# The later modulation products of a diffusion backbone, row sums on VectorE and one matmul per unit on TensorE

## The chip, the core and the metric

The kernel runs on one core of one Trainium2 chip. The metric is the device time of one execution in microseconds (us). Before the change the median of 3 runs is 3228.99 us (3227.17 to 3229.79). Everything is float32. The engines are TensorE (PE), VectorE (DVE), ScalarE (ACT), GpSimd (POOL) and SyncE (SP); POOL and SP here mostly issue DMAs.

## The reference, cut to what matters

Two layers, each a mixer and a mixture of single-neuron experts ("PEER") over 512 latent tokens of width 1024; layer 0's mixer also reads 256 context tokens. Every sub-layer is modulated by a shift, a scale and a gate that come from the conditioning vector:

```python
silu_c = jax.nn.silu(c)                       # c: (1, 1024)
for l in range(DEPTH):                        # DEPTH = 2
    sh1, sc1, g1, sh2, sc2, g2 = jnp.split((silu_c @ ada_w[l] + ada_b[l])[:, None, :], 6, axis=-1)
    h = modulate(x, sh1, sc1)                 # rms_norm(x) * (1 + sc1) + sh1
    ...                                       # even: attention and spatial gating; odd: convolution
    x = x + g1 * y
    x = x + g2 * peer_ffn(modulate(x, sh2, sc2), peer_wq[l], peer_keys[l], peer_down[l], peer_up[l])
```

`ada_w[l]` is 1024 by 6144. So the modulation is a product of one row of 1024 numbers with 2 times 25 MB of weights (`c_ctx` needs a part of layer 0's as well). `peer_ffn` picks 128 experts for each token and gathers their down and up rows (1024 numbers each); that is most of the kernel's DMA.

## The kernel before, in words

**Stages.** The plan (`make_plan`, L520) writes one order of stage phases; each engine walks it and takes from it its own part (`run_phases`, L757). Ahead of the first expert gather stands the front, some 270 us: norms and projections of all tokens, layer 0's mixer for block 0 (128 tokens), the choice of its experts, and the whole modulation. Then come 8 stretches of 128 gathers (4 blocks, 2 layers), with the other blocks' mixers and choices spread between them (`beside`, L422). The order in the front is the text `FRONT` (L512): a word is a stage's letter and a phase. `k`, `q` and `v` are projections, `g` the gating, `a` the attention (23 phases of `ATTEND`, L458), `p` the output projection and the update of x, `n` the norm for the experts, `s` the choice of experts, `u` and `w` modulation products and `t` and `y` their transposition. Inside the front all engines have the same order.

**Modulation.** The weights come in halves: 512 columns of 512 of the 1024 rows, 1 MB, in SBUF as 128 partitions of 4 rows by 512 columns. Two halves are a unit (`unit`, L182), which is 512 outputs of one section; a section has 1024 outputs, so 2 units. There are three groups of units (`side`, L195): 4 units for the first norms, 6 (`u`), and the last 14 units, 28 halves, `w0` to `w27` in `FRONT`. GpSimd issues the halves' DMAs in order (L823), five to eight ahead: the DMA for a half waits on the count `side_used`, which says how many products have been read out of the buffers. For a half TensorE runs 4 matmuls (L1595), one for each of the 4 rows, into the 4 groups of 32 output partitions, with `cond_slide` as the stationary operand: 32 columns of zeros with the conditioning numbers in two of them, moved so that unit m adds to row 2m of each group. After the last half ScalarE copies the 128 by 512 sums to SBUF (`turned`, L889), TensorE sums the four groups and transposes in one (4 matmuls with `chosen`, L1607) and VectorE adds the biases (L1215).

**What is around it.** `attend` on VectorE takes row maxima of the scores (`peaks`, L1312) and mixes the two softmaxes (`combine`, L1319); ScalarE waits for the first with its exponentials and TensorE for the second with a transposition. `gating` on VectorE: `bn_stats` (L1287), the normalisation (L1292 to L1296) and the product (L1303). `project` on VectorE: two passes of 1024 columns (L1354, L1356) that update x; ScalarE then squares and sums x, VectorE takes the reciprocal (L1228), scales x (L1229), TensorE transposes, VectorE and ScalarE modulate one half each (L1236, L958). After that TensorE starts the choice's projections (L1578), and the first gathers follow.

Of the kernel before, what the change touches and what calls it, by code (L numbers as in the profile page):

```python
# [18 lines left out]
ALU = mybir.AluOpType  # L19
# [3 lines left out]
P = 128  # L23
# [90 lines left out]
class Plan:  # L114
# [80 lines left out]
    def side(self, sections):  # L195

        units = [self.unit(layer, sec, j, 2 * n + j) for n, (layer, sec) in enumerate(sections) for j in range(2)]
        sums = Stage("side", parts=units, cost=(1,) * (2 * len(units)))
        turned = Stage("turned", parts=sections, cost=(1, 1))
        sums.group = turned.group = self.groups  # L200
# [315 lines left out]
p3 p4 p5 n0 w24 w25 n1 w26 w27 n2 y0 n3 s0 y1 s1 s2 s3 s4 s5 s6 s7  # L516
# [3 lines left out]
def make_plan():  # L520
# [46 lines left out]
    rest, rest_turned = p.side([(1, SH1), (1, SC1), (1, G1), (1, SH2), (1, SC2), (1, G2), (0, G2)])  # L567
# [24 lines left out]
def trunk_kernel(nc, A, out):  # L592
    plan = make_plan()
    with ExitStack() as ctx:
# [58 lines left out]
        diag = sb("diag", [P, RING, HALF])  # L653
        psum = ctx.enter_context(nc.psum_tensor("psum", [P, 4, 2 * COLS], F32))
# [69 lines left out]
        side_used, side_line = sem("side_used"), sem("side_line")  # L724
        side_out, side_done = sem("side_out"), sem("side_done")
# [133 lines left out]
        def _(act):  # L859
# [277 lines left out]
        def _(dve):  # L1137
# [26 lines left out]
            dve.memset(cond_slide, 0.0).then_inc(consts, 1)  # L1164
            dve.wait_ge(first_params, 48)
# [25 lines left out]
            def lam(s):  # L1191
# [9 lines left out]
                                              op0=ALU.add, op1=ALU.subtract))  # L1201
                yield
# [318 lines left out]
            run_phases({"turned": turned, "front_norms": front_norms, "lam": lam, "norm": norm, "heads": heads, "gating": gating, "attend": attend, "project": project,  # L1521
# [4 lines left out]
        def _(pe):  # L1526
# [54 lines left out]
            def side(s):  # L1581
# [4 lines left out]
                elif s.group == 2:  # L1586

                    pe.wait_ge(side_line, 1)
# [9 lines left out]

            def turned(s):
# [268 lines left out]
```

## Time and profile before

| | us |
|---|---|
| median of 3 runs | 3228.99 (3227.17 to 3229.79) |
| span of the profiled execution (first to last instruction) | 3226.1 |
| its own run time | not listed apart from the three runs |
| TensorE busy | 2352.4 (73%) |
| VectorE busy | 2215.5 (69%) |
| ScalarE busy | 1284.6 (40%) |
| GpSimd busy | 1194.8 (37%) |
| DMA, 1286.05 MB | mean 399 GB/s |

The span runs from the first to the last instruction; the median of the runs stands 2.9 us above it. Busy shares are averages over unlike stages: the front is short, 8% of the span, and has other limits than the gathers. The chain that ended last is 33% DMA, 31% TensorE, 20% VectorE and 8% ScalarE.

### The profile page before, as it was taken

How to read it: one execution, taken by the hardware profiler on the slowest of the kernel's cores; microseconds unless marked ns; L12 is line 12 of the kernel's file. 1: busy time of each engine (PE TensorE's matmuls, PEld its weight loads, DVE VectorE, ACT ScalarE, POOL GpSimd, SP SyncE). 2: the span in 40 equal slices, each digit the busy share in tenths (PEclk: the TensorE clock that was granted, in tenths of full speed). 3: DMA queues.
4: the chain of work that ended last, by engine and by line, in shares of the span. 5: the costliest groups of instructions: out<-in, count | busy, mean ns of one | idle time of the engine just before them, and what ended most of it. 6: DMA issues, size and time to landing. Idle time of an engine off the chain costs nothing.

```text
span 3226.1 us, 38561 instructions
## 1 busy us (share of the span) xinstructions
PE 2352.4 (73%) x13032; PEld 919.0 (28%) x13032; DVE 2215.5 (69%) x5652; ACT 1284.6 (40%) x3707; POOL 1194.8 (37%) x1076
## 2 busy tenths in 40 slices
PE   6997778576775878876685796956686667867776
PEld 2335225122341235431151251511143112511110
DVE  2325875866568655869849968599948996795444
ACT  3223463345434553533434534333343433443333
POOL 1102343433334342335433434335433453344332
PEclk9998789688887888887797796967688667966666
DMA  8778999999999999999999999999999999999998
GB/s 333 260 300 344 415 375 423 410 398 406 410 422 414 418 401 421 391 422 410 419 404 416 401 418 420 392 404 397 421 399 421 405 421 391 421 399 422 421 421 357
DMA packets 169766, 1286.05 MB, mean 399 GB/s; under 512 B 19552, under 2 KB 20448, under 8 KB 23392
## 3 DMA queue, kind: packets, MB, share of 16 engines
q0 software_dynamic: 154368, 1124.14, 85.4%
q1 hardware_dynamic: 15200, 159.45, 11.9%
q8 instruction: 102, 1.67, 0.2%
q14 instruction: 96, 0.79, 0.1%
HBM read 1281.42 MB, written 2.10 MB: 398 GB/s over the span
## 4 chain that ended last, share of the span: by engine, by line
DMA 33%; PE 31%; DVE 20%; ACT 8%; issue 7%; POOL 1%; DVEq 0%; SPq 0%; ACTq 0%; POOLq 0%
DMA ring<-in_experts,expert 32%; PE psum L1798 11%; DVE ring L1500 8%; PE psum L1564 7%; PE psum L1578 4%; PE psum L1744 4%; DVE arena L1391 2%; PE psum L1536 1%; PE psum L1595 1%; ACT shares_of L1128 1%; ACT diag L1129 1%; DVE arena L1419 1%; PE psum L1550 1%; ACT acts L1127 1%; ACT L1127 1%
## 5 line engine op out<-in xcount | busy, mean ns | idle before, releaser
L1798 PE MATMUL psum<-ring,diag 64*64 64x512 f32 x8192 | 1430.3, 805 | 746.7 <-ACT diag L1129 739.8
L852 POOL DMA_INDIRECT ring<-in_experts,expert x1024 | 1169.0, 1142 | 1807.0 <-PE psum L1798 1666.0
L1500 DVE CUSTOM_DVE_ANT_0 ring<-ring,h 128x1024 f32<-128x1024 f32 x1024 | 1230.9, 1223 | 530.3 <-DMA ring<-in_experts,expert 499.9
L1127 ACT ACTIVATE acts<-dots 128x1 f32<-128x1 f32 x1024 | 206.7, 202 | 1475.0 <-DVE dots L1500 1431.4
L1798 PEld LDWEIGHTS psum<-ring,diag 64*64 64x64 f32 x8192 | 286.4, 162 | 1719.5 <-ACT diag L1129 1519.6
L1129 ACT ACTIVATE diag<-ident_half,shares_of 128x64 f32<-128x64 f32 x1024 | 356.4, 348 | 33.3
L1128 ACT ACTIVATE shares_of<-acts,gate 128x1 f32<-128x1 f32 x1024 | 302.0, 295 | 33.3
L1391 DVE SCALAR_TENSOR_TENSOR arena<-kept,taps,arena 128x128 f32<-128x128 f32 x960 | 262.6, 345 | 0.1
L1578 PEld LDWEIGHTS psum<-arena,weights 128*128 128x128 f32 x2048 | 234.2, 192 | 48.9 <-issue 47.0
L1578 PE MATMUL psum<-arena,weights 128*128 128x128 f32 x2048 | 245.7, 278 | 0.1
L878 ACT ACTIVATE arena<-psum 128x512 f32<-128x512 f32 (+1 forms) x105 | 65.5, 624 | 206.0 <-PE psum L1578 119.6
L1564 PE MATMUL psum<-weights,arena 128*128 128x512 f32 x272 | 135.5, 644 | 4.7 <-ACTq L962 4.7
L1744 PE MATMUL psum<-arena,weights 128*128 128x256 f32 x512 | 119.1, 386 | 0.4 <-ACTq L962 0.4
L1564 PE MATMUL psum<-weights,ring 128*128 128x512 f32 x240 | 112.2, 612 | 3.7 <-ACTq L917 3.7
L1536 PE MATMUL psum<-ident,arena 128*128 128x128 f32 x464 | 81.2, 328 | 35.4 <-DVEq L1396 8.1
L1744 PEld LDWEIGHTS psum<-arena,weights 128*128 128x128 f32 x512 | 94.6, 190 | 38.6 <-issue 24.4
L1127 ACT ACT_TABLE_LOAD x78 | 100.1, 1283 | 6.0 <-ACT arena L1034 2.0
L833 POOL DMA_DIRECT2D ring<-in_chunks x46 | 24.5, 535 | 198.4 <-PE psum L1595 167.8
L1536 PEld LDWEIGHTS psum<-ident,arena 128*128 128x128 f32 x464 | 64.0, 168 | 101.5 <-issue 50.1
L1316 DVE TENSOR_REDUCE peak<-psum 128x1 f32<-128x768 f32 x32 | 30.5, 952 | 80.6 <-PE psum L1691 80.4
L1500 DVE DVE_READ_ACCUMULATOR2_ANT dots<- 128x1 f32 x1024 | 84.1, 82 | 0.0
L1564 PEld LDWEIGHTS psum<-weights,arena 128*128 128x128 f32 x272 | 53.3, 207 | 86.4 <-issue 80.0
(166 smaller groups left out, 1519.3 us busy)
## 6 DMA issues: line engine op xcount, KB each, us to landing
weights<-in_chunks SPq DMA_DIRECT2D x70, 2048.0 KB
ring<-in_chunks POOLq DMA_DIRECT2D x46, 1024.0 KB, 7.2
ring<-in_experts,expert POOLq DMA_INDIRECT x1024
arena<-in_chunks SPq DMA_DIRECT2D x10, 512.0 KB
x<-in_x SPq DMA_DIRECT2D x1, 2048.0 KB, 19.8
kept<-in_chunks POOLq DMA_DIRECT2D x2, 1024.0 KB, 19.9
out_x<-x SPq DMA_DIRECT2D x4, 512.0 KB
ring<-in_ctx SPq DMA_DIRECT2D x1, 1024.0 KB, 9.6
```

What stands on the lines that cost most here:

```text
L852: pool.indirect_dma_start(out=ring[:, k, :], out_offset=None, in_=table, in_offset=bass.IndirectOffsetOnAxis(ap=expert[:, s.b % 2, n:n + 1 ...
L878: step(act.activation(dst, src, ACT.Copy))
L1127: step(act.activation(acts[:, k:k + 1], dots[:, k:k + 1], ACT.Gelu))
L1128: step(act.activation(shares_of[:, k:k + 1], acts[:, k:k + 1], ACT.Copy, scale=gate[:, s.b % 2, n:n + 1]))
L1129: act.activation(diag[:, k, :], ident_half[:], ACT.Copy, scale=shares_of[:, k:k + 1]).then_inc(diag_ready, 1)
L1391: dve.scalar_tensor_tensor(out=acc[:, k, :], in0=z_t[:, k, w + s.b * P:w + (s.b + 1) * P], scalar=taps[:, k, w:w + 1], in1=acc[:, k, :], o ...
L1500: dve.tensor_tensor_reduce(out=ring[:, k, 0:D], in0=ring[:, k, 0:D], in1=h2[:, s.b % 2, :], scale=1.0, scalar=0.0, op0=ALU.mult, op1=ALU.a ...
L1536: ins = pe.transpose(psum[:, t.bank, k * P:(k + 1) * P], src[:, k * P:(k + 1) * P], ident[:])
L1564: ins = pe.matmul(dst, left[:, k, :], buffers[c.buf][:, k, :], start=k == 0 and begin, stop=k == KD - 1, skip_group_check=not begin)
L1578: ins = pe.matmul(dst, buffers[c.buf][:, k, g * P:(g + 1) * P], right[:, k, :], start=k == 0, stop=k == KD - 1)
L1744: ins = pe.matmul(psum[:, t.bank, 2 * g * P:2 * (g + 1) * P], buffers[c.buf][:, k, g * P:(g + 1) * P], h_pair[:, k, :], start=k == 0, stop ...
L1798: pe.matmul(ffn_out[rows_out, r * COLS:(r + 1) * COLS], diag[rows_in, k, :], ring[rows_in, k, D + n * COLS:D + (n + 1) * COLS], start=Fals ...
```

## The change

The last group's 28 halves are no longer multiplied on TensorE. VectorE keeps one 128 by 512 tile per unit: it multiplies the first row of the first half with the conditioning number of each partition (one `tensor_scalar`) and adds the other seven rows, each times its number (seven `scalar_tensor_tensor`). Each of these waits for the one before it through `side_used`, which GpSimd waits on too. There are two such tiles, a new one and the tile `diag`, which is not in use before the gathers. When a unit is whole, TensorE adds up the partitions with one matmul of 32 output rows (`one_slide`: zeros with a column of ones) into the bank. The stage has 30 phases in place of 28: TensorE's matmul for unit m stands in phase 2m + 3, VectorE's work for the unit's halves in phases 2m and 2m + 1. At the end ScalarE copies 32 rows in place of 128 and TensorE transposes with 32 rows of the identity. The first two groups stay as they are.

```diff
-    def side(self, sections):
+    def side(self, sections, added=False):
+        before = len(self.units)
         units = [self.unit(layer, sec, j, 2 * n + j) for n, (layer, sec) in enumerate(sections) for j in range(2)]
-        sums = Stage("side", parts=units, cost=(1,) * (2 * len(units)))
+        sums = Stage("added" if added else "side", parts=units, cost=(1,) * (2 * len(units) + (2 if added else 0)))
...
-p3 p4 p5 n0 w24 w25 n1 w26 w27 n2 y0 n3 s0 y1 s1 s2 s3 s4 s5 s6 s7
+p3 p4 p5 n0 w24 w25 n1 w26 w27 n2 w28 w29 y0 n3 s0 y1 s1 s2 s3 s4 s5 s6 s7
...
-    rest, rest_turned = p.side([(1, SH1), (1, SC1), (1, G1), (1, SH2), (1, SC2), (1, G2), (0, G2)])
+    rest, rest_turned = p.side([(1, SH1), (1, SC1), (1, G1), (1, SH2), (1, SC2), (1, G2), (0, G2)], added=True)
...
+        one_slide = sb("one_slide", [P, 62])
+        added_to = [sb("added_to", [P, COLS])[:], diag[:].rearrange("p s n -> p (s n)")]
...
             def turned(s):
-                act.wait_ge(side_used, s.used)
                 if s.group == 2:
                     act.wait_ge(side_out, 1)
-                act.activation(lines[s.group], side_bank[s.group], ACT.Copy).then_inc(side_line, 1)
+                    act.wait_ge(side_summed, s.added)
+                    act.activation(lines[s.group][0:32, :], side_bank[s.group][0:32, :], ACT.Copy).then_inc(side_line, 1)
+                else:
+                    act.wait_ge(side_used, s.used)
+                    act.activation(lines[s.group], side_bank[s.group], ACT.Copy).then_inc(side_line, 1)
...
+            def added(s):
+                dve.wait_ge(cond_act, 1)
+                used = s.before
+                for u in s.parts:
+                    dst = added_to[u.m % 2]
+                    if u.m > 1:
+                        dve.wait_ge(side_summed, u.m - 1)
+                    for h, (buf, there, _) in enumerate(u.halves):
+                        dve.wait_ge(side_landed[buf], there)
+                        for k in range(KD // 2):
+                            dve.wait_ge(side_used, used)
+                            share = cond_slide[:, 4 * h + k, 30:31]
+                            if h + k == 0:
+                                ins = dve.tensor_scalar(dst, side_bufs[buf][:, k, :], share, None, ALU.mult)
+                            else:
+                                ins = dve.scalar_tensor_tensor(out=dst, in0=side_bufs[buf][:, k, :], scalar=share, in1=dst,
+                                                               op0=ALU.mult, op1=ALU.add)
+                            ins.then_inc(side_used, 1)
+                            used += 1
+                        if h:
+                            dve.wait_ge(side_used, used)
+                            dve.sem_inc(side_added, 1)
+                        yield
+                yield
+                yield
...
+            def added(s):
+                yield
+                yield
+                yield
+                pe.wait_ge(side_line, 1)
+                pe.wait_ge(one_ready, 2)
+                for u in s.parts:
+                    at = 30 - 2 * u.m
+                    pe.wait_ge(side_added, u.m + 1)
+                    pe.matmul(side_bank[s.group][0:32, :], one_slide[:, at:at + 32], added_to[u.m % 2], start=u.m == 0,
+                              stop=True, skip_group_check=True).then_inc(side_summed, 1)
+                    yield
+                    yield
...
+                rows, turn_by = (32, ident[0:32, 0:32]) if s.added else (P, chosen[:])
                 for g in range(4):
-                    ins = pe.matmul(dst[:, 32 * g:32 * (g + 1)], lines[s.group][:, g * P:(g + 1) * P], chosen[:], start=True, stop=True)
+                    ins = pe.matmul(dst[:, 32 * g:32 * (g + 1)], lines[s.group][0:rows, g * P:(g + 1) * P], turn_by, start=True, stop=True)
```

How this moves the instructions is seen at three places. In the rows `waits` names the counts that an instruction waits for; the new kernel's lines on VectorE stand 40 further down than the old ones (L1316 is L1356 there), and its `added` is L1231 and L1233.

First, VectorE around the last pair of score maxima of the front's attention. Before, from the gating's statistics to the gating's product:

```order
L1287 BN_STATS stats<-psum 128x6 [waits psum_full1]
L1288 BN_AGGR meanvar<-stats 128x2 [waits dve_step]
L1292 RECIPROCAL rstd_v<-std_v 128x1 [waits std_ready]
L1293 TENSOR_SCALAR g2_row<-psum,meanvar,rstd_v 128x512 [waits dve_step]
L1295 TENSOR_TENSOR g2_row<-g2_row,vn_gain 128x512 [waits dve_step]
L1296 TENSOR_TENSOR g2_row<-g2_row,vn_gain 128x512 [waits dve_step]
L1316 TENSOR_REDUCE peak<-psum 128x1 [waits psum_full0]
```

Now the same stretch from the end of the gating's normalisation, up to the gating's product:

```order
L1336 TENSOR_TENSOR g2_row<-g2_row,vn_gain 128x512 [waits dve_step]
L1233 SCALAR_TENSOR_TENSOR diag<-ring,arena,diag 128x512 [waits side_used,side_landed0]
L1233 SCALAR_TENSOR_TENSOR diag<-ring,arena,diag 128x512 [waits side_used] x3
L1356 TENSOR_REDUCE peak<-psum 128x1 [waits side_used,psum_full0]
L1357 TENSOR_SCALAR neg_peak<-peak 128x1 [waits dve_step]
L1356 TENSOR_REDUCE peak<-psum 128x1 [waits psum_full1]
L1357 TENSOR_SCALAR neg_peak<-peak 128x1 [waits dve_step]
L1231 TENSOR_SCALAR added_to<-ring,arena 128x512 [waits side_used,side_landed1,side_summed]
L1233 SCALAR_TENSOR_TENSOR added_to<-ring,arena,added_to 128x512 [waits side_used] x3
L1362 RECIPROCAL inv_sum<-expsum 128x2 [waits exp_ready]
```

Four operations (half `w19`) now stand ahead of the maxima, and four (`w20`) between the maxima and the mix.

Second, VectorE from the update of x to the modulation of the experts' input. Before:

```order
L1356 TENSOR_TENSOR x<-x,arena 128x1024 [waits dve_step]
L1228 RECIPROCAL rstd<-std 128x1 [waits std_ready]
L1229 TENSOR_SCALAR arena<-x,rstd 128x1024 [waits dve_step]
L1236 TENSOR_SCALAR arena<-psum,mod 128x128 [waits mod_ready,psum_full2]
L1236 TENSOR_SCALAR arena<-psum,mod 128x128 x3
```

Now:

```order
L1396 TENSOR_TENSOR x<-x,arena 128x1024 [waits dve_step]
L1231 TENSOR_SCALAR added_to<-ring,arena 128x512 [waits side_used,side_landed0,side_summed]
L1233 SCALAR_TENSOR_TENSOR added_to<-ring,arena,added_to 128x512 [waits side_used] x3
L1233 SCALAR_TENSOR_TENSOR added_to<-ring,arena,added_to 128x512 [waits side_used,side_landed1]
L1233 SCALAR_TENSOR_TENSOR added_to<-ring,arena,added_to 128x512 [waits side_used] x3
L1268 RECIPROCAL rstd<-std 128x1 [waits side_used,std_ready]
L1269 TENSOR_SCALAR arena<-x,rstd 128x1024 [waits dve_step]
L1231 TENSOR_SCALAR diag<-ring,arena 128x512 [waits side_used,side_landed2,side_summed]
L1233 SCALAR_TENSOR_TENSOR diag<-ring,arena,diag 128x512 [waits side_used] x3
L1233 SCALAR_TENSOR_TENSOR diag<-ring,arena,diag 128x512 [waits side_used,side_landed3]
L1233 SCALAR_TENSOR_TENSOR diag<-ring,arena,diag 128x512 [waits side_used] x3
L1276 TENSOR_SCALAR arena<-psum,mod 128x128 [waits side_used,mod_ready,psum_full2]
```

Eight operations (`w24`, `w25`) now stand between the update of x and the reciprocal, and eight (`w26`, `w27`) between the scaled x and its modulation.

Third, TensorE around the scores of head 2 (L1691 before, L1744 now). Before:

```order
L1595 MATMUL psum<-ring,arena 32x512 [waits side_landed8]
L1595 MATMUL psum<-ring,arena 32x512 x3
L1691 MATMUL psum<-kept,arena 128x512 [waits psum_free0]
L1691 MATMUL psum<-kept,arena 128x256
L1691 MATMUL psum<-kept,arena 128x512 [waits psum_free1]
L1691 MATMUL psum<-kept,arena 128x256
L1595 MATMUL psum<-ring,arena 32x512 [waits side_landed0]
L1595 MATMUL psum<-ring,arena 32x512 x3
L1707 MATMUL psum<-kept,arena 128x128 [waits psum_free2,probst_ready,v_ready]
```

Now:

```order
L1646 MATMUL psum<-diag,one_slide 32x512 [waits side_added]
L1744 MATMUL psum<-kept,arena 128x512 [waits psum_free0]
L1744 MATMUL psum<-kept,arena 128x256
L1744 MATMUL psum<-kept,arena 128x512 [waits psum_free1]
L1744 MATMUL psum<-kept,arena 128x256
L1760 MATMUL psum<-kept,arena 128x128 [waits psum_free2,probst_ready,v_ready]
```

Four matmuls for every half became one for every second half, and it waits for VectorE (`side_added`) where the four waited for a DMA (`side_landed`).

## Rows read from the trace of the kernel before

**Rows 1.** Busy time in four stretches: length, engines, granted TensorE clock, DMA share, GB/s.
```profile
117.00:184.50 67.50, 65.92 (x272) 25.86 (x270) 11.71 (x25) 13.77 (x23) 7.42 (x14) 1.00 0.71 253
184.50:238.00 53.50, 50.67 (x240) 23.32 (x242) 14.29 (x29) 14.11 (x23) 4.77 (x9) 1.00 0.80 322
238.00:290.00 52.00, 37.75 (x300) 30.98 (x300) 18.19 (x62) 12.03 (x23) 9.35 (x9) 0.90 0.74 294
290.00:3226.00 2936.00, 2111.34 (x11888) 803.28 (x11880) 2135.22 (x5453) 1211.72 (x3571) 1159.65 (x1015) 0.78 0.99 409
```

**Rows 2.** Chain of waits, front: start us, us, what.
```profile
117.41 1.85 PE psum L1595 x16
...
178.44 3.63 PE psum L1564 x8
...
222.49 1.00 PE psum L1595 x8
...
228.45 1.00 PE psum L1595 x8
```

**Rows 3.** VectorE's groups by shape, first 290 us: busy us, mean ns of one.
```profile
L1270 DVE TENSOR_TENSOR arena<-arena,rope_cos 128x512 f32<-128x512 f32 x5 | 3.5, 691 | 0.2
L1174 DVE TENSOR_SCALAR arena<-x,rstd 128x1024 f32<-128x1024 f32 x4 | 2.7, 748 | 0.0
...
L1198 DVE TENSOR_SCALAR subln<-subln 128x128 f32<-128x128 f32 x1 | 0.2, 217 | 0.0
```

**Rows 4.** The page's costliest groups, the convolution's taps.
```profile
L1391 DVE SCALAR_TENSOR_TENSOR arena<-kept,taps,arena 128x128 f32<-128x128 f32 x960 | 262.6, 345 | 0.1
```

**Rows 5.** VectorE in order of time: start us, us, what, idle before.
```profile
197.00 0.70 DVE L1287 BATCH_NORM_STATS2 stats<-psum 128x6 f32<-128x512 f32 x1 [7.31 <-PE psum L1564]
...
198.28 0.16 DVE L1292 RECIPROCAL rstd_v<-std_v 128x1 f32<-128x1 f32 x1 [0.36 <-ACT std_v L1016]
198.47 0.81 DVE L1293 TENSOR_SCALAR g_row<-psum,meanvar,rstd_v 128x512 f32<-128x512 f32 x1
199.43 0.69 DVE L1295 TENSOR_TENSOR g_row<-g_row,vn_gain 128x512 f32<-128x512 f32 x1
...
208.73 0.96 DVE L1316 TENSOR_REDUCE peak<-psum 128x1 f32<-128x768 f32 x1 [7.88 <-PE psum L1691]
...
213.92 0.17 DVE L1322 RECIPROCAL inv_sum<-expsum 128x2 f32<-128x2 f32 x1 [2.99 <-ACTq L1038]
...
214.37 1.02 DVE L1325 SCALAR_TENSOR_TENSOR arena<-arena,inv_sum 128x768 f32<-128x768 f32 x1
215.31 1.12 DVE L1303 SCALAR_TENSOR_TENSOR arena<-psum,sgu_bias,g_row 128x128 f32<-128x128 f32 x4
225.57 0.69 DVE L1336 TENSOR_TENSOR arena<-arena 128x512 f32<-128x512 f32 x1 [9.14 <-ACTq L1053]
...
227.35 0.18 DVE L1341 RECIPROCAL rstd<-std 128x4 f32<-128x4 f32 x1 [0.37 <-ACT std L1056]
...
239.38 1.23 DVE L1356 TENSOR_TENSOR x<-x,arena 128x1024 f32<-128x1024 f32 x1
242.15 0.16 DVE L1228 RECIPROCAL rstd<-std 128x1 f32<-128x1 f32 x1 [1.54 <-ACT std L949]
...
244.29 1.37 DVE L1236 TENSOR_SCALAR arena<-psum,mod 128x128 f32<-128x128 f32 x4 [1.19 <-PE psum L1536]
```

**Rows 6.** TensorE in order of time, the same columns.
```profile
217.27 1.25 PE L1536 MATMUL psum<-ident,arena 128*128 128x128 f32 x10
...
229.38 0.66 PE L1536 MATMUL psum<-ident,arena 128*128 128x128 f32 x4
...
245.99 1.09 PE L1536 MATMUL psum<-ident,arena 128*128 128x128 f32 x8 [1.74 <-ACTq L962]
```

**Rows 7.** GpSimd's DMAs of the halves, line 833.
```profile
DMA to landing us min/median/max: 5.1/7.8/23.7
```

**Rows 8.** GpSimd's first gather, in order of time, the same columns.
```profile
270.06 0.99 POOL L852 DMA_INDIRECT ring<-in_experts,expert  x1 [45.65 <-issue]
```

More of the change, by code:

```diff
@@ L193, in unit @@
         return u
-    def side(self, sections):
+    def side(self, sections, added=False):
+        before = len(self.units)
         units = [self.unit(layer, sec, j, 2 * n + j) for n, (layer, sec) in enumerate(sections) for j in range(2)]
-        sums = Stage("side", parts=units, cost=(1,) * (2 * len(units)))
+        sums = Stage("added" if added else "side", parts=units, cost=(1,) * (2 * len(units) + (2 if added else 0)))
         turned = Stage("turned", parts=sections, cost=(1, 1))
+        sums.before, turned.added = 8 * before, len(units) if added else 0
         sums.group = turned.group = self.groups
@@ L724, in trunk_kernel @@
         side_used, side_line = sem("side_used"), sem("side_line")
+        one_ready = sem("one_ready")
+        side_added, side_summed = sem("side_added"), sem("side_summed")
         side_out, side_done = sem("side_out"), sem("side_done")
@@ L1164, in _ @@
             dve.memset(cond_slide, 0.0).then_inc(consts, 1)
+            dve.memset(one_slide[:], 0.0).then_inc(one_ready, 1)
+            dve.wait_ge(one_ready, 1)
+            dve.memset(one_slide[:, 30:31], 1.0).then_inc(one_ready, 1)
             dve.wait_ge(first_params, 48)
@@ L1519, in finish @@
                 yield
-            run_phases({"turned": turned, "front_norms": front_norms, "lam": lam, "norm": norm, "heads": heads, "gating": gating, "attend": attend, "project": project,
+            run_phases({"added": added, "turned": turned, "front_norms": front_norms, "lam": lam, "norm": norm, "heads": heads, "gating": gating, "attend": attend, "project": project,
                         "conv_in": conv_in, "conv": conv, "select": select, "gather": gather, "finish": finish}, "others")
@@ L1585, in side @@
                     pe.wait_ge(side_done, 1)
-                elif s.group == 2:
-                    pe.wait_ge(side_line, 1)
                 bank = side_bank[s.group]
@@ L1805, in _ @@
             pe.wait_ge(consts, 4)
-            run_phases({"side": side, "turned": turned, "front_norms": front_norms, "norm": norm, "heads": heads, "values": values, "gate_row": gate_row, "gating": gating, "attend": attend,
+            run_phases({"side": side, "added": added, "turned": turned, "front_norms": front_norms, "norm": norm, "heads": heads, "values": values, "gate_row": gate_row, "gating": gating, "attend": attend,
                         "project": project, "conv_in": conv_in, "conv": conv, "select": select, "gather": gather}, "pe")
```

## The prediction

> **What bounds the kernel now.** I read the busy time by stretch first [rows 1]. From 290 us to the end the DMA share is 0.99: the gathers set the pace there, and the change doesn't touch them. So it can only move the time at which they start. In the front the DMA share is 0.71 to 0.80, while TensorE is busy for 65.92 of 67.50 us and 50.67 of 53.50: it bounds the front to about 205 us. VectorE is busy for 11.71 and 14.29 us in the same two stretches. TensorE's granted clock is 1.00 in both, its upper level, so there is no clock to win back. Then I read the chain of waits [rows 2]: between 117 and 230 us the products of the halves stand on it, w0 and w1 as one piece of 1.85 us, 18 pieces of 1.00 (w2 to w19), and w22 and w23: 21.85 us. w20 and w21 run while TensorE would wait for ScalarE, w24 to w27 while x is updated and normed. Last, VectorE in order of time [rows 5]: after 205 us the front is a chain of short steps over three engines, with VectorE idle until each of its steps is due.
>
> **What is removed and added.** TensorE loses 28 halves of 1.00 us and gets 14 single matmuls of 128 by 32 by 512. No row shows one alone. A full-width matmul of 512 columns takes 3.63 / 4 = 0.91 us; a quarter of a half's four, which run side by side, is 0.25; all four are 1.00 [rows 2]. I take 0.91, since all 512 columns pass through either way, and keep 0.25 and 1.00 as bounds. The Trainium skill (TensorE: Matmul & The Clock Gate, "Why this matters for your kernels") says of small outputs that each should lie in a column group of its own so that they run at once, 2.38 times faster for three; the packed 1.00 us agrees, and a lone one would then cost about what four do. By 0.91 the ten that are not hidden cost 9.1 us, so TensorE alone would give back 21.85 - 9.1 = 12.8 us.
>
> VectorE gets, per unit, one `tensor_scalar` and seven `scalar_tensor_tensor`, each waiting for the last. The latter is not in the trace at 128 by 512. At 768 columns it takes 1.02 us [rows 5]; between the taps' 128 columns (0.345) [rows 4] and that the slope is 0.675 / 640 = 1.05 ns a column, so 1.02 - 256 x 1.05 ns = 0.75, with 0.03 until a dependent operation starts (198.44 to 198.47) [rows 5]: 0.78. Bounds: 0.69 as for a two-source operation of that size [rows 3], and 1.02. The `tensor_scalar`: 0.217 at 128 columns and 0.748 at 1024 [rows 3] make 0.44 at 512, with the gap 0.48 (bounds 0.22 and 0.75). A first half is then 0.48 + 3 x 0.78 + 0.03 for its extra waits = 2.85, a second 4 x 0.78 + 0.12 for the count it raises (199.28 to 199.43 less the usual gap) = 3.25. A unit is 6.1, all 14 are 85 us, and they must go into some 120 us in which VectorE already works for 26 [rows 1]. There is just room, so what matters is where each half stands in VectorE's order.
>
> **Step by step**, new times against old ones.
> 1. To the end of head 2's scores (184.5): TensorE loses w0 to w13, 1.85 + 12 x 1.00 = 13.85 us, and gets 6 x 0.91 = 5.5. VectorE needs 5.7 to 6.1 us for a unit that TensorE takes 8.2 for (two pieces of 3.63 and one of 0.91), and stands idle in most of the stretch [rows 1], so it keeps up. New end: 176.1 (saved 8.4).
> 2. From here VectorE is full. Maxima 2.2 us (two of 0.96 and two small ones), w14 2.85, mix 1.5 (213.92 to 215.39), w15 3.25, w16 2.85, the gating's statistics 0.95, w17 3.25, w18 2.85, its normalisation 2.6 (198.28 to 199.43 and two passes of 0.73), w19 3.25: 25.6 us. The maxima of head 3 start at 201.75, where TensorE by itself would have its scores at 197.0 (24.2 us in the old trace, less six halves, plus three single matmuls). Old: 208.73 [rows 5]. Saved: 7.0.
> 3. The mix follows 5.2 us later, set by ScalarE (208.73 to 213.92), w20 hides in it. But w21 (3.25) stands between the mix (1.5) and the gating's product (1.12), and TensorE's transposition waits for that product: 201.75 + 5.2 + 1.5 + 3.25 + 1.12 + 0.1 = 212.9, old 217.27 [rows 5, 6]. Saved: 4.4.
> 4. w22 leaves TensorE (1.0) and a wait of 0.25 closes; the squares start at 219.9 (old 225.57). Behind them come 1.42 us, w23 with 3.25, then 1.63 from 227.35 [rows 5]: the transposition at 226.3, old 229.38 [rows 6]. Saved: 3.1.
> 5. The projection is as before, so the second pass over x starts at 239.38 - 3.1 and ends at 237.5. VectorE then does w24 and w25, 6.1 us, ahead of the reciprocal: 243.6, old 242.15. The cover (ScalarE's squares) is 1.5 us and no more. Lost: 1.5.
> 6. It scales x (0.95), does w26 and w27 (6.1), and modulates from 250.65, old 244.29 [rows 5]. The cover here is 1.2 us. The first projection of the experts' choice, behind the transposition at 245.99 [rows 6], is 6.4 us late.
> 7. From there all is as before, one to one: ScalarE's copy of the sums and TensorE's transposition stand in the same places, and unit 13's matmul (251.6) is done before ScalarE asks. The gathers start 6.4 us late and stay late, at a DMA share of 0.99.
>
> Costed at nothing: the new constants at the start, hidden by the first loads; GpSimd's DMAs, which are now released by VectorE. A half's landing takes 7.8 us in the median [rows 7], they are issued five halves ahead, and VectorE takes 3 us for one; a landing like the longest, 23.7 us, would stop VectorE and all that is queued behind, maxima and mixes included.
>
> **The sum** is made against the profiled execution: span 3226.1 + 6.4 = 3232.5. The median of the runs stands 2.9 above the span: 3228.99 + 6.4 = 3235.4; I say 3235.5, 0.2% slower. A difference under 0.2% (6.46 us) can't be told from no change, so this lies on the border. Sensitivity: 43 `scalar_tensor_tensor` and 5 `tensor_scalar` stand on the path (w14 to w19, w21, w23 to w27). At 0.69 + 0.03 in place of 0.78 the sum is 6.4 - 2.6 = +3.8; at 1.02 + 0.03 it is +18. The `tensor_scalar`'s bounds give -1.1 and +1.5. A single matmul at 0.25 gives -4 over the six of step 1, at 1.00 +0.5.
>
> **Rivals.**
> - *TensorE's time decides.* VectorE's halves hide wholly, and the front gives back 12.8 us: 3216. For it: VectorE is idle for four fifths of the front [rows 1]. Against: it works in order, and four halves stand in a tail where its waits are 1.2 and 1.5 us [rows 5]. It would take halves that end before the update of x.
> - *The chained operations run at the taps' pace.* These come every 262.6 / 960 = 0.274 us for 128 columns [rows 4], 0.67 at 512 by the slope. For it: same operation, also with counts. Against: eight independent ones lie between dependent taps, and here each waits. Then 43 x 0.11 = 4.7 less: +1.7, 3230.7. The Trainium skill (Vector Engine (DVE) Microarchitecture Reference, 5.2 Measured stream behaviour) gives 1.0417 ns a column and about 75 ns an instruction after overlap; an estimate by that is 0.61 us and a sum of about -0.9, still no change that can be told.
> - *Halves come late to VectorE.* In w14 to w19 and the tail VectorE consumes in bursts (6.1 us for two), and GpSimd's DMA is issued only when the whole buffer is read; a landing above 15 us, while SyncE's 2 MB chunks load too, halts VectorE ahead of the maxima. Two or three such halts of 3 us: 3243. Against: DMA share 0.71 to 0.80 [rows 1]. It decides from the point where a landing takes five halves' time, 15 us.
> - *The shift is swallowed later.* Then 3229. Against: DMA share 0.99 after 290 us.
>
> **How the numbers follow.** VectorE's tail as summed, with small unshown waits that rather add: 0.76, own range 3231 to 3241, of it 0.43 above 3235.45 and 0.33 below. Taps' pace 0.06, TensorE decides 0.09, late halves 0.07, swallowed 0.02. So faster 0.09, within 0.2% 0.41, slower 0.50. The range for 8 in 10 leaves out most of the case at 3216: 3226 to 3243.
>
> **What would show it.** A step is right if: TensorE's head-2 scores end near 176; the maxima of head 3 start near 202 with VectorE busy without a gap before; the reciprocal after the update of x waits for VectorE's own work, not ScalarE; the experts' first gather is issued near 276.5, old 270.06 [rows 8]. `scalar_tensor_tensor` at 128 by 512 should read 0.75 us and follow every 0.78; the single matmuls should come as 0.91. The forecast is wrong if the first gather comes before 270, if VectorE waits for DMAs of the halves, or if the first gather's shift and the shift of the end differ by more than 2 us.

## The result, and the profile after

The changed kernel takes 3238.19 us (median of 5 runs, 3236.24 to 3239.95), the kernel before 3227.17 us in the same comparison (5 runs, 3221.39 to 3229.79). The ratio is 1.0036, 95% interval 1.0025 to 1.0047: slower by 0.36%, 11.0 us. The forecast was 3235.5 us and 0.2%, with a range of 3226 to 3243 us. The profiled execution took 3236.24 us, with a span of 3234.4.

First the stretches. The last three rows are 5 us long.

Changed kernel, busy time by stretch (columns as in [rows 1]):

```profile
116.00:176.40 60.40, 57.21 (x172) 24.97 (x170) 48.34 (x77) 13.76 (x23) 7.44 (x14) 1.00 0.78 285
176.40:238.00 61.60, 52.01 (x167) 26.18 (x166) 42.68 (x70) 14.10 (x23) 4.81 (x9) 0.89 0.72 280
...
290.00:3234.00 2944.00, 2115.27 (x11912) 809.85 (x11912) 2139.37 (x5457) 1212.66 (x3577) 1157.08 (x1017) 0.78 0.99 409
205.00:210.00 5.00, 3.64 (x17) 3.00 (x18) 4.64 (x8) 2.21 (x5) 0.53 (x1) 0.59 0.98 410
225.00:230.00 5.00, 3.13 (x7) 1.61 (x8) 0.98 (x2) 0.60 (x1) 0.00 (x0) 0.64 0.00 0
245.00:250.00 5.00, 3.71 (x10) 1.75 (x10) 4.68 (x8) 0.00 (x0) 0.00 (x0) 0.50 0.01 2
```

The gathers run as before, at a DMA share of 0.99 [rows 1]; what changed lies in the front. There VectorE went from 11.71 us of 67.50 to 48.34 of 60.40. What the forecast did not have is in the clock column: [rows 1] shows 1.00 up to 238 us, and now it is 0.89 between 176.4 and 238, and in the three short stretches 0.59, 0.64 and 0.50. A granted clock of 0.5 is TensorE's lower level, 1.2 GHz, and 1.00 is 2.4 GHz; a value between them is a stretch with some of both.

Changed kernel, VectorE's groups by shape, 110 to 290 us (columns as in [rows 3], the last the idle time before and its releaser):

```profile
L1233 DVE SCALAR_TENSOR_TENSOR diag<-ring,arena,diag 128x512 f32<-128x512 f32 x49 | 36.8, 751 | 1.7
...
L1231 DVE TENSOR_SCALAR diag<-ring,arena 128x512 f32<-128x512 f32 x7 | 3.4, 485 | 1.8 <-DVE added_to L1233 1.1 <-DVE arena L1343 0.3 <-DVE mod L1255 0.3
```

Each of the two tiles got half of the 98 chained operations. They take 0.751 us (forecast 0.75), the first of a unit 0.485 (0.44).

Changed kernel, VectorE in order of time, a choice of rows that answers to [rows 5]:

```profile
198.27 3.11 DVE L1233 SCALAR_TENSOR_TENSOR diag<-ring,arena,diag 128x512 f32<-128x512 f32 x4
201.52 0.96 DVE L1356 TENSOR_REDUCE peak<-psum 128x1 f32<-128x768 f32 x1
...
208.10 3.11 DVE L1233 SCALAR_TENSOR_TENSOR added_to<-ring,arena,added_to 128x512 f32<-128x512 f32 x4
211.42 1.12 DVE L1343 SCALAR_TENSOR_TENSOR arena<-psum,sgu_bias,g_row 128x128 f32<-128x128 f32 x4 [0.21 <-DVE added_to L1233]
...
237.60 1.22 DVE L1394 TENSOR_TENSOR arena<-psum,g_row 128x1024 f32<-128x1024 f32 x1 [11.60 <-PE psum L1590]
238.97 1.23 DVE L1396 TENSOR_TENSOR x<-x,arena 128x1024 f32<-128x1024 f32 x1
...
240.63 5.54 DVE L1233 SCALAR_TENSOR_TENSOR added_to<-ring,arena,added_to 128x512 f32<-128x512 f32 x7
246.32 0.16 DVE L1268 RECIPROCAL rstd<-std 128x1 f32<-128x1 f32 x1
...
247.70 5.54 DVE L1233 SCALAR_TENSOR_TENSOR diag<-ring,arena,diag 128x512 f32<-128x512 f32 x7
253.46 1.37 DVE L1276 TENSOR_SCALAR arena<-psum,mod 128x128 f32<-128x128 f32 x4 [0.22 <-DVE diag L1233]
```

Before, the maxima of head 3 (now L1356), the reciprocal (L1268) and the modulation (L1276) waited for another engine, 7.88, 1.54 and 1.19 us [rows 5]. Now the first two follow VectorE's own work without a wait, and the modulation waits 0.22 us for it, as the gating's product (L1343) does. L1233 stands right ahead of each. The seven operations at 240.63 are the ones that come ahead of the reciprocal (246.32), those at 247.70 the ones ahead of the modulation (253.46).

Changed kernel, TensorE in order of time, which answers to [rows 2] and [rows 6]:

```profile
118.24 1.08 PE L1660 MATMUL psum<-chosen,h 128*128 128x32 f32 x8 [1.61 <-ACT h L903]
...
173.87 1.05 PE L1646 MATMUL psum<-diag,one_slide 128*32 128x512 f32 x2
174.84 1.57 PE L1744 MATMUL psum<-kept,arena 64*128 64x512 f32 x8
...
201.49 1.04 PE L1646 MATMUL psum<-diag,one_slide 128*32 128x512 f32 x2 [1.50 <-DVEq L1239]
205.22 1.41 PE L1730 MATMUL psum<-g_row,sgu_t 128*128 128x128 f32 x8 [2.69 <-ACTq L1046]
...
212.75 1.31 PE L1576 MATMUL psum<-ident,arena 128*128 128x128 f32 x10 [0.54 <-DVEq L1348]
...
226.07 0.83 PE L1576 MATMUL psum<-ident,arena 128*128 128x128 f32 x4 [2.41 <-DVE arena L1384]
227.70 9.87 PE L1590 MATMUL psum<-weights,arena 128*128 128x512 f32 x16 [0.80 <-ACTq L886]
...
246.29 1.92 PE L1646 MATMUL psum<-added_to,one_slide 128*32 128x512 f32 x2 [7.74 <-DVEq L1239]
...
255.04 1.97 PE L1576 MATMUL psum<-ident,arena 128*128 128x128 f32 x8
```

The releaser `DVEq` or `ACTq` is that engine's sequencer. A float32 matmul has two records, so x2 is one matmul. The kernel before has these two rows, the second group's last product and the projection:

```profile
112.27 1.07 PE L1595 MATMUL psum<-ring,arena 128*32 128x512 f32 x8
...
230.84 7.13 PE L1550 MATMUL psum<-weights,arena 128*128 128x512 f32 x16 [0.80 <-ACTq L880]
```

TensorE now stands still where its own halves used to fill the time: 1.50 us at 201.49, 2.69 at 205.22, 2.41 at 226.07, 7.74 at 246.29, 3.25 at 253.35. And its work is slower right behind the waits: the 16 records of the projection at 227.70 take 9.87 us (7.13 before, at 230.84), the transposition of 8 records at 255.04 takes 1.97 us in place of 1.09 [rows 6].

Changed kernel, landing of the halves (line 839 now), and GpSimd's first gather, which answer to [rows 7] and [rows 8]:

```profile
DMA to landing us min/median/max: 5.2/6.5/23.5
```

```profile
280.41 0.99 POOL L858 DMA_INDIRECT ring<-in_experts,expert  x1 [63.85 <-issue]
```

The first gather is issued at 280.41 us, 10.35 later than before.

**A common zero.** Executions differ by up to 1.5 us in when they reach the stretch that was changed, so I count from the start of the second group's last product (four packed matmuls, 8 records, at 112.27 us before, 111.49 after). "Front" is from there to the first gather. Differences to before:

| us against before | forecast | after |
|---|---|---|
| maxima of head 2 (184.5) | -8.4 | -7.4 |
| maxima of head 3 | -7.0 | -6.4 |
| transposition for `p0` | -4.4 | -3.7 |
| transposition after the squares | -3.1 | -2.5 |
| second pass over x | -3.1 | +0.4 |
| reciprocal | +1.5 | +5.0 |
| modulation | +6.4 | +10.0 |
| first gather | +6.4 | +11.1 |

The front's 11.1 us and the time's 11.0 us go one to one. Of the 4.7 us between forecast and measurement, 2.9 come in one step, the projection between the transposition and the second pass over x, and 1.1 behind the modulation.

### The profile page after: what moved, and what is told of

It reads as the page before. It is cut to its first block, busy times and chain, and to the rows that moved or that the text cites. A ratio compares the mean times of both kernels' runs of the same rounds, so it can differ in the third digit from the quotient of the medians.

```text
span 3234.4 us, 38325 instructions
## 1 busy us (share of the span) xinstructions
PE 2345.7 (73%) x12836; PEld 925.1 (29%) x12836; DVE 2295.8 (71%) x5766; ACT 1283.8 (40%) x3707; POOL 1190.4 (37%) x1076
## 4 chain that ended last, share of the span: by engine, by line
DMA 32%; PE 29%; DVE 22%; issue 8%; ACT 7%; POOL 1%; DVEq 0%; SPq 0%; ACTq 0%; POOLq 0%
DMA ring<-in_experts,expert 31%; PE psum L1851 10%; DVE ring L1540 8%; PE psum L1604 6%; PE psum L1618 4%; PE psum L1797 4%; DVE arena L1431 3%; PE psum L1576 1%; POOL ring L858 1%; PE psum L1590 1%; ACT diag L1138 1%; ACT shares_of L1137 1%; DVE arena L1459 1%; ACT L1117 1%; ACT acts L1136 1%
## 5 line engine op out<-in xcount | busy, mean ns | idle before, releaser
L1394 DVE TENSOR_TENSOR arena<-psum,g_row 128x1024 f32<-128x1024 f32 x8 | 9.8, 1224 | 90.8 <-PE psum L1604 63.9
```

## The experiments

Two theories stand against each other. *Clock*: the four steps that VectorE now stands ahead of cost what the forecast says, and the rest is TensorE's clock, which fell because TensorE waits. *VectorE alone*: the whole loss is VectorE's work in the way, and the clock costs nothing. Each kernel ran beside the kernel before on the same chip, the first four and the last four together. The kernel before had a median of 3226.88 us (29 runs) and of 3227.19 (27 runs). The changed kernel's row is taken from the result above. The stages come from one profiled execution of each kernel. The expectations number their theories each for itself. Stages are counted from the zero above, ratios are to the kernel before.

| kernel | ratio (95%) | median us | maxima head 3 | second pass | modulation | front |
|---|---|---|---|---|---|---|
| before | 1 | 3227.2 | 96.46 | 127.11 | 132.02 | 157.79 |
| after | 1.0036 (1.0025 to 1.0047) | 3238.19 | 90.03 | 127.48 | 141.97 | 168.92 |
| tail_early | 1.0010 (1.0000 to 1.0020) | 3229.50 | 90.04 | 128.59 | 134.36 | 161.95 |
| tail_skipped | 0.9994 (0.9984 to 1.0005) | 3225.22 | 90.04 | 127.55 | 133.07 | 159.03 |
| vector_skipped | 0.9968 (0.9956 to 0.9981) | 3215.80 | 86.25 | 115.69 | 121.53 | 147.61 |
| filled | 1.0027 (1.0017 to 1.0037) | 3236.85 | 90.04 | 125.94 | 140.44 | 168.05 |
| filled_more | 1.0021 (1.0012 to 1.0029) | 3233.99 | 90.03 | 124.58 | 139.07 | 165.03 |
| split7 | 0.9974 (0.9963 to 0.9985) | 3218.26 | 89.92 | 120.58 | 125.49 | 151.27 |
| split9 | 0.9976 (0.9965 to 0.9987) | 3219.72 | 89.39 | 120.05 | 124.96 | 150.72 |
| split9_later | 0.9981 (0.9973 to 0.9990) | 3221.63 | 91.80 | 122.45 | 127.36 | 154.53 |

### tail_early: the last four halves ahead of the update of x

```diff
-p3 p4 p5 n0 w24 w25 n1 w26 w27 n2 w28 w29 y0 n3 s0 y1 s1 s2 s3 s4 s5 s6 s7
+p3 w24 w25 p4 w26 w27 p5 n0 w28 n1 w29 n2 y0 n3 s0 y1 s1 s2 s3 s4 s5 s6 s7
```

> The last four halves (w24 to w27) move ahead of the update of x in the order of all engines, into the 11.6 us in which VectorE waits for the projection; nothing is left out. Theory 1 (VectorE's halves stand in the way where the other engines wait 1.2 and 1.5 us): the update of x starts at about 238.4, the reciprocal follows it after 1.5 us and the modulation after another 2.1, so the first gather is issued at 270 to 272 in place of 280.4, and the time is 8 to 10 us under the changed kernel's, within 2 us of the kernel before. Theory 2 (TensorE's low clock alone, from its idle times in the attention): the order in the tail matters little, the first gather comes at 277 or later. Theory 3 (the loss sits behind the front): the first gather moves but the time does not.

The kernel tail_early, VectorE around the update of x, in order of time:

```profile
234.17 5.55 DVE L1233 SCALAR_TENSOR_TENSOR diag<-ring,arena,diag 128x512 f32<-128x512 f32 x7
239.93 1.22 DVE L1394 TENSOR_TENSOR arena<-psum,g_row 128x1024 f32<-128x1024 f32 x1 [0.21 <-DVE diag L1233]
...
244.07 0.16 DVE L1268 RECIPROCAL rstd<-std 128x1 f32<-128x1 f32 x1 [1.54 <-ACT std L958]
...
247.07 1.37 DVE L1276 TENSOR_SCALAR arena<-psum,mod 128x128 f32<-128x128 f32 x4 [2.05 <-PE psum L1576]
```

Units 12 and 13 now lie in VectorE's wait for the projection, which is 11.60 us in the changed kernel (at 237.60). They take some 12.4 us and overfill it by little: the update at 239.93 waits 0.21 us for them. The reciprocal waits for ScalarE again (1.54), as in [rows 5]. The front falls from 168.92 to 161.95 us: 7.0 of the 11.1 us are where those four halves stand. The time is 8.7 us under the changed kernel's, as expected, but 2.6 us above the kernel before where 2 was the most. The first gather was expected at 270 to 272 us and came at 274.66 (273.4 with the changed kernel's zero): a miss by 1.4 us. Against the kernel before the second pass is 1.5 late, the modulation 2.3, the first gather 4.2; the modulation waits here for a transposition of 1.95 us at a clock of 0.51:

```profile
245.00:250.00 5.00, 3.19 (x14) 2.79 (x15) 1.39 (x5) 2.09 (x5) 0.00 (x0) 0.51 0.10 13
```

### tail_skipped: units 12 and 13 leave out VectorE's chained operations

```diff
                         for k in range(KD // 2):
+                            if u.m >= 12 and h + k:
+                                dve.sem_inc(side_used, 1)
+                                used += 1
+                                continue
```

Of the last two units the sums hold only the first row of eight; the rest of the work and of the order is that of the changed kernel.

> Of the last two units (w24 to w27) VectorE only does the first row; the other fourteen operations are left out and only counted, so these outputs are not the reference's. Theory 1: 14 times 0.78 = 10.9 us leave VectorE's order behind the update of x; of these 3 us were covered before, so the first gather comes 8 to 9 us earlier, at 271 to 272.5, and the time falls by as much, to that of the kernel before. Theory 2 (low clock): at most 3 us earlier, 277 or later.

The kernel tail_skipped, VectorE in order of time:

```profile
242.60 0.16 DVE L1272 RECIPROCAL rstd<-std 128x1 f32<-128x1 f32 x1 [1.15 <-ACT std L958]
...
245.36 1.37 DVE L1280 TENSOR_SCALAR arena<-psum,mod 128x128 f32<-128x128 f32 x4 [1.40 <-DVEq L1231]
```

A hit (first gather 271.32). The reciprocal and the modulation each have a wait for another engine again, so what stood ahead of them was the price. 14 operations of 0.79 are 11.1 us; the modulation comes 8.9 us earlier, and the other 2.2 lay in waits. The front is 9.9 us shorter, because another 1.0 comes behind the modulation, where the clock is 1.00 from 245 to 250 us and the second transposition takes 1.09 us. Yet the front is still 1.2 us longer than before, although it had a lead of 6.4 us at head 3's maxima. That lead goes at w21, w23 and in the projection, which takes 9.96 us here too.

### vector_skipped: all units leave them out

```diff
+                            if h + k:
+                                dve.sem_inc(side_used, 1)
+                                used += 1
+                                continue
```

The modulation's last group holds one row of eight. TensorE's part is that of the changed kernel.

> Of each unit VectorE only does the first row; the other 98 operations are left out and only counted, so the later modulation is not the reference's. TensorE, the DMAs and the waits stay. This is the rival in which TensorE's time decides. If TensorE's removed time is really given back when VectorE is free, the update of x starts near 225.5 (12.5 us before the old 238.0, less 1.6 us for the wait ahead of the transposition of the second group), the first gather is issued at 257 to 260 and the time is 3215 to 3219. If it stays above 265, something other than VectorE (the halves' DMAs, ScalarE) holds the front.

The front is 10.2 us shorter than before and the time 0.32% less, 3215.80: a hit, and what TensorE alone gives back. It is the forecast's rival at 3216. VectorE's 98 operations, with the clock that falls when TensorE waits for them, are what lies between it and the 3238.19 measured. TensorE still waits here, but the projection has its full clock (7.13 us), and the granted clock is 1.00 in every 5 us from 175 to 230 us. Behind a wait of 2.98 us ahead of unit 12's matmul it is 0.66 (230 to 235 us), and the transposition there takes 1.97 us.

### filled: matmuls without a use in TensorE's waits

```diff
+                def fill(n):
+                    for _ in range(n):
+                        pe.matmul(side_b, ident[:], sgu_t[:].rearrange("p g n -> p (g n)"), start=True, stop=True)
+                ahead, behind = {9: 2, 12: 0, 13: 3}, {9: 3, 10: 3, 11: 9}
...
+                    fill(ahead.get(u.m, 0))
                     pe.wait_ge(side_added, u.m + 1)
                     pe.matmul(side_bank[s.group][0:32, :], one_slide[:, at:at + 32], added_to[u.m % 2], start=u.m == 0,
                               stop=True, skip_group_check=True).then_inc(side_summed, 1)
+                    fill(behind.get(u.m, 0))
```

The fillers, 0.89 us each (nine, 18 records, in 7.99 us behind unit 11), write into a bank half that is free by then, and nothing reads them.

> TensorE gets 20 matmuls of 128 by 512 whose result nobody reads, where it waits in the tail: 5 around w21, 3 behind w23, 9 behind w25, 3 ahead of w29. Theory 2 (TensorE's idle times from 200 us on lower its clock, and that makes the projection 9.9 us long in place of 7.1): the granted clock stays 1.00 to 255 us, the projection takes 7.1 and the update of x starts 2.7 us earlier, the first gather at about 276.5, 3.5 to 4 us earlier. If the long projection has another cause (a late weight chunk, contention), the filling changes nothing or costs up to 2 us.

The kernel filled, TensorE in order of time:

```profile
213.09 2.40 PE L1576 MATMUL psum<-ident,arena 128*128 128x128 f32 x10 [2.53 <-DVEq L1348]
...
229.21 7.13 PE L1590 MATMUL psum<-weights,arena 128*128 128x512 f32 x16 [0.80 <-ACTq L886]
...
252.14 1.05 PE L1655 MATMUL psum<-diag,one_slide 128*32 128x512 f32 x2 [2.32 <-DVEq L1239]
253.84 1.88 PE L1576 MATMUL psum<-ident,arena 128*128 128x128 f32 x8 [0.65 <-ACTq L971]
```

The projection at 229.21 takes 7.13 us, so its 9.87 were the clock. But two waits, of 2.53 and 2.32 us, were left unfilled, and behind them the clock is 0.76 to 0.90: the 10 records take 2.40 us (1.25 before [rows 6]) and the 8 take 1.88. A miss: the front fell by 0.9 us where some 4 were expected, since what the projection gained was in part lost ahead of it and behind the modulation.

### filled_more: the same with those two waits filled

```diff
-                ahead, behind = {9: 2, 12: 0, 13: 3}, {9: 3, 10: 3, 11: 9}
+                ahead, behind = {9: 2, 13: 6}, {9: 3, 10: 2, 11: 9}
...
+                            for _ in range(2 if s.b == 0 else 0):
+                                pe.matmul(side_b, ident[:], sgu_t[:].rearrange("p g n -> p (g n)"), start=True, stop=True)
```

The two of the last lines stand in `project`, ahead of TensorE's wait for the gating's product.

> The changed kernel with TensorE's waits of the tail filled more closely than before: 5 matmuls without use around w21, 2 ahead of the transposition of the gating's part, 2 behind w23, 9 behind w25, 6 ahead of w29. In the first filling two waits of 2.3 to 2.5 us were left and the clock fell to 0.8 after each. If idle time of TensorE is what lowers the clock, it is now 1.00 from 195 to 260 us, the projection starts where it did in the changed kernel (within 0.5 us) and takes 7.1, and the front from the second group's last product to the first gather is 164.5 to 166 us in place of 168.9 (first filling: 168.05). If it stays at 168 or more, the low clock is not worth what its rows say.

The kernel filled_more, busy time by stretch, and TensorE in order of time:

```profile
225.00:230.00 5.00, 3.70 (x12) 1.52 (x11) 1.83 (x4) 0.60 (x1) 0.00 (x0) 1.00 0.00 0
245.00:250.00 5.00, 5.00 (x19) 2.59 (x18) 4.72 (x8) 1.50 (x4) 0.00 (x0) 1.00 0.00 2
```

```profile
228.56 7.13 PE L1590 MATMUL psum<-weights,arena 128*128 128x512 f32 x16 [0.80 <-ACTq L886]
...
253.18 1.09 PE L1576 MATMUL psum<-ident,arena 128*128 128x128 f32 x8 [0.46 <-ACTq L971]
```

A hit. The clock is 1.00 in every 5 us from 195 to 265, the projection takes 7.13 us, the last transposition 1.09. The front is 165.03 us, 3.9 less than the changed kernel's, with VectorE's order and work untouched. The forecast's front was 157.8 + 6.4 = 164.2. So the clock was worth 3.9 of the 4.7 us that the forecast missed, and VectorE alone is refuted as the whole cause. The times point the same way, 11.0 us above the kernel before for the changed kernel and 6.8 for this one, but their intervals overlap (1.0025 to 1.0047 and 1.0012 to 1.0029); the proof is in the rows. The fall isn't a chance of one execution: tail_skipped, with the same waits ahead of its projection as the changed kernel, takes 9.96 us for it, and the six kernels in which the wait of 2.41 us ahead of it is filled or gone (0.49 us at most) take 7.13.

### split7 and split9: VectorE takes the first 7 or 9 units, TensorE the others

```diff
-                for u in s.parts:
+                for u in s.parts[:7]:
...
+                    if 2 * by_vector <= phase < 2 * len(s.parts):
+                        u, h = s.parts[phase // 2], phase % 2
...
+                        for k in range(KD // 2):
+                            pe.matmul(bank[32 * k:32 * (k + 1), :], cond_slide[:, 4 * h + k, at:at + 32], side_bufs[buf][:, k, :],
+                                      start=u.m == by_vector and h == 0 and k > 0, stop=True, skip_group_check=True).then_inc(side_used, 1)
```

TensorE goes on with the packed matmuls of the kernel before, into the same bank; ScalarE copies 128 rows again. With 9 in place of 7 it is split9.

> VectorE takes only the first 7 of the 14 units (w0 to w13, where it stood idle), TensorE multiplies the other 7 as in the kernel before; the transposition sums the four groups again. Theory 1 (the loss is where the halves stand in VectorE's order, not what they cost): from the last product of the second group to the first gather the kernel before takes 157.8 us and the changed one 168.9; here 13.9 us leave TensorE, 7 single matmuls of 0.97 and the 1.6 us wait ahead of the second group's transposition come, so 152.5 to 153.5, and the time is 4 to 6 us under the kernel before. The granted clock stays 1.00 from 117 to 260 us. Theory 2 (VectorE's products slow the front as such, through the halves' DMAs or the counts): 158 or more.

> The same with 9 of 14 units on VectorE (to w17). VectorE then does w14 to w17 in the stretch of the gating, and has 2 us left before the maxima of head 3. Theory 1: 4 more us leave TensorE for two more single matmuls (1.9 us), front from the second group's last product to the first gather 150.5 to 151.5 us, the time 6 to 8 us under the kernel before. If the maxima of head 3 wait for VectorE after all, it gives back those 2 us and is like the one with 7.

The kernel split7, VectorE in order of time, and TensorE:

```profile
201.94 0.96 DVE L1358 TENSOR_REDUCE peak<-psum 128x1 f32<-128x768 f32 x1 [7.88 <-PE psum L1756]
...
231.23 1.23 DVE L1396 TENSOR_TENSOR arena<-psum,g_row 128x1024 f32<-128x1024 f32 x1 [9.03 <-PE psum L1592]
...
235.37 0.16 DVE L1270 RECIPROCAL rstd<-std 128x1 f32<-128x1 f32 x1 [1.54 <-ACT std L959]
```

```profile
179.40 0.62 PE L1649 MATMUL psum<-added_to,one_slide 128*32 128x512 f32 x1
179.41 0.63 PE L1659 MATMUL psum<-ring,arena 128*32 128x512 f32 x3
...
224.06 7.13 PE L1592 MATMUL psum<-weights,arena 128*128 128x512 f32 x16 [0.80 <-ACTq L886]
231.13 3.64 PE L1659 MATMUL psum<-ring,arena 128*32 128x512 f32 x32
```

VectorE has a wait of 9.03 us for the projection, and those of 7.88 and 1.54 us as before the change [rows 5], and TensorE's halves fill its own waits: 32 records at 231.13 lie in the update of x. The clock is 1.00 from 117 to 265 us. The lead at head 3's maxima, 6.5 us, reaches the first gather whole (151.27 against 157.79), and the time is 3218.26 us: faster than both kernels. The front was to be 152.5 to 153.5 us and is 1.2 to 2.2 better; the time was to be 4 to 6 us under the kernel before and is 8.9.

The kernel split9, TensorE in order of time:

```profile
192.53 1.07 PE L1659 MATMUL psum<-ring,arena 128*32 128x512 f32 x8 [1.01 <-DVE added_to L1234]
...
237.84 1.09 PE L1578 MATMUL psum<-ident,arena 128*128 128x128 f32 x8 [1.74 <-ACTq L972]
```

A hit (front 150.72, time 7.5 us under the kernel before). But two more units on VectorE save only 0.55 us of front against split7, and nothing that the time shows. Their last half is late for w18: TensorE waits 1.01 us for it.

### split9_later: split9 with w2 ahead of the query's chain

```diff
-q0 u11 q1 t0 k12 w0 w1 t1 w2 v0 q2 q3 q4 v1 r0 q5 a0 w3 a1 v2 w4 a2 v3 a3 w5 a4 v4 w6 a5 v5 w7 a6 v6 w8 v7 w9 v8 w10 v9 w11 v10 w12
+q0 u11 q1 t0 k12 w0 w1 v0 t1 w2 q2 q3 q4 v1 r0 q5 a0 w3 a1 v2 w4 a2 v3 a3 w5 a4 v4 w6 a5 v5 w7 a6 v6 w8 v7 w9 v8 w10 v9 w11 v10 w12
```

> As with 9 units, and the second group's transposition is moved behind the first half of the values' projection, so that TensorE does not wait 1.6 us for ScalarE's copy. Theory 1: 1.6 us less than with 9 units, unless VectorE's later start of the query's chain takes it back: front 149 to 151 us, time 7 to 10 us under the kernel before.

The kernel split9_later, VectorE and TensorE in order of time:

```profile
121.13 0.31 DVE L1257 SCALAR_TENSOR_TENSOR mod<-psum,ada_bias 128x8 f32<-128x8 f32 x3 [2.22 <-PE psum L1672]
```

```profile
129.41 0.66 PE L1578 MATMUL psum<-ident,arena 128*128 128x128 f32 x4 [3.02 <-DVE arena L1320]
130.87 2.94 PE L1756 MATMUL psum<-kept,arena 64*128 64x512 f32 x8 [0.80 <-ACTq L886]
...
240.59 1.97 PE L1578 MATMUL psum<-ident,arena 128*128 128x128 f32 x8 [1.74 <-ACTq L972]
```

A miss. I wanted to cover the 1.61 us wait for ScalarE's copy that the changed kernel has at 118.24. It is covered, by a value projection of 3.7 us, but VectorE's next step waits for the transposition behind that (2.22 us at 121.13), the query's chain comes later, TensorE stands 3.02 us at 129.41, and the scores behind take 2.94 us in place of 1.57. The front is 3.8 us longer than split9's. Of that 2.4 us are there at head 3's maxima, and 1.4 come behind the modulation: from 240 to 245 us the clock is 0.66, and the second transposition takes 1.97 us (240.59) where split9, with the same wait of 1.74 us ahead of it, takes 1.09 (237.84).

## Why the prediction came out as it did

**Sign and place: right.** The forecast said that the front loses what VectorE does in order ahead of four steps of the tail, more than TensorE gives back. tail_early and tail_skipped show it: moving those halves takes 7.0 us off the front, leaving their operations out 9.9. Of the signs that the forecast named, these came: head 2's scores end at 176.34, head 3's maxima start at 201.52 behind VectorE's own work, the reciprocal waits for VectorE's own work, the operation takes 0.751 us and follows every 0.79. These did not: a single matmul takes 0.97 us, and the first gather comes at 280.41 in place of 276.5.

**Step 1, -8.4, measured -7.4.** Three errors, of which the last goes the other way. A single matmul of 32 output rows takes 0.97 us, not 0.91 (six: 0.4 us). Without w0 and w1 TensorE waits 1.61 us for ScalarE at 118.24, so these 1.85 us gave almost nothing; I had counted them whole and not asked what they covered. Against these, a half between two projection pieces costs more than its 1.00: 16 records in one piece take 7.07 us until the next piece starts (142.07 to 149.14 in the changed kernel), two pieces of 3.63 take 7.26, which gives 0.2 back five times.

**Steps 2 to 4, right in size.** The durations of [rows 5] and the extrapolated 0.75 gave VectorE's order within 0.6 us: from head 2's maxima to head 3's the forecast had 25.65 us (176.1 to 201.75), measured are 25.1. The halves landed in time (5.2, 6.5 and 23.5 us at least, median and most); VectorE waited for no DMA, so the rival of late halves did not happen.

**Step 5, wrong: "The projection is as before."** It took 9.87 us for 7.13. The sentence behind it is in the first part: "TensorE's granted clock is 1.00 in both, its upper level, so there is no clock to win back." I read the clock only as something to win. By step 2 the forecast itself had TensorE done at 197.0 and VectorE's maxima at 201.75, which is idle time on an engine whose clock, as filled_more shows, depends on its work. The missing term is that clock: 2.7 us in the projection, 0.9 in the transposition at 255.04 (1.97 for 1.09) and 0.3 in what follows it, 3.9 by filled_more. The Trainium skill (TensorE: Matmul & The Clock Gate, "The HAM clock gate") says that the array runs at 1.2 GHz when TensorE has been idle and comes back after it has been busy; the rows of this case agree (0.59 from 205 to 210 us behind waits of 1.50 and 2.69 us, 1.00 there with the fillers), and it would have put a rival beside the others.

**Steps 5 and 6 for VectorE: right.** From the second pass to the reciprocal and on to the modulation the forecast had +4.6 and +4.9 us, measured +4.6 and +5.0.

**Step 7, "one to one": nearly.** From the modulation to the first gather 26.95 us now, 25.77 before; filled_more has 25.96 with VectorE's work the same. That 1.0 is the clock too. From the first gather to the end it is one to one within the intervals: the eight experiments lie between -10.2 and +10.3 us of front and between -0.32% and +0.27% of time, in nearly the same order.

**The sum.** Forecast +6.4 us; measured 11.1 = 6.4 + 0.8 (what is left, for the most part step 1) + 3.9 (clock). That 3238.19 us lies even inside the narrower range for VectorE's tail, 3231 to 3241, is in part luck: the range was kept for small waits on VectorE, and the larger part of the miss, the clock, was no term of it. Two of the three signs set as "the forecast is wrong if" did not come up. The third, shifts of the first gather and of the end more than 2 us apart, came up by a hair in the profiled execution (10.35 and 8.3); its run was the fastest of five, and over the medians the end moved by 11.0.

**What stays open.** The clock is 0.59 to 0.72 between 205 and 215 us and costs nothing there, since VectorE sets the pace: the transposition for `p0` comes 101.26 us behind the zero in the changed kernel and in filled_more. When TensorE's idle time makes the clock fall is not settled by these runs. split9 and split9_later have the same row of waits and matmuls from the projection on (1.62 and 1.74 us ahead of the two transpositions), and one keeps 1.00 while the other falls to 0.66.

## What to carry to other kernels

Work that an in-order engine takes over costs what stands behind it there, so compare each piece with the wait that is to cover it: here one of 11.60 us lay unused beside two of 1.2 and 1.5 that were overfilled. Where work leaves TensorE, list the waits that it had filled; these come back as idle time, and the clock behind them may fall. Share the work at the point where the helper is full (7 of 14 units) rather than move it whole: that kept TensorE's gain, 6.5 us of 7.4, and its clock.

## What the runs showed of the hardware

- One matmul of 128 rows, 32 output rows and 512 columns takes 0.97 us until the next starts (173.87 to 174.84), about what four packed ones take (1.00): the other three cost 0.03 us. The Trainium skill (TensorE: Matmul & The Clock Gate, "Why this matters for your kernels") has column groups run at once, and the measurement agrees.
- Packed matmuls begin beside a single one: in split7 the rows at 179.40 to 179.87 hold the two records of a single matmul and eight of a half, and all are through at 181.24, 1.84 us later, where one after the other they would be 1.97.
- The chained operation, each waiting for the last, comes every 0.79 us at 512 columns (0.75 of its own); seven take 5.54 us.
- Behind the count raised at the end of a unit VectorE stands for 0.21 or 0.22 us before its next operation (211.42 and 253.46 in the changed kernel, 239.93 in tail_early).
